# Gate ranks in one chunk, decays by bias on ScalarE, one AND for the causal mask, and a reordered start

## The reference

```python
h = rmsnorm(x_lat, norm1_g[i]) * (1.0 + sc1) + sh1          # sc1, sh1: from silu(c) @ ada_w
log_gate = log_sigmoid((lr @ gate_w[d] + gate_b[d])) / GLA_TAU   # lr: 16 columns of h @ w_in per direction
# linear attention, chunks of 64 tokens, forward and backward, 4 heads
b = cumsum(g)                                   # within the chunk
qe, ke, kd = q * exp(b), k * exp(-b), k * exp(b_last - b)
att = where(mask, qe @ ke.T, 0);  o = att @ v + qe @ S
S = exp(b_last) * S + kd.T @ v
# latent attention, 8 heads: softmax(q @ k.T) @ v; then pooling, three gated branches, w_out
# PEER: for each token and each of 8 heads the top 16 of 16384 experts
out = sum_j softmax(top)_j * gelu(x . u[eid_j]) * v[eid_j]
```

## Time and profile before

| what | value |
|---|---|
| median of 3 runs | 3509.55 us (3503.07 to 3510.31) |
| profiled execution, its own time | 3512.18 us |
| span of the profiled execution | 3510.2 us |
| PE, PE weight load | 2868.5 us, 1793.2 us busy |
| VectorE, ScalarE, GpSimd | 1751.3 us, 1083.8 us, 862.1 us busy |
| HBM read | 1067.80 MB |

### The profile page before, as it was taken

The page is one execution under the profiler, slowest core; times in us unless marked ns, Lnnn a source line. Parts: engine busy times, 40 slices in busy tenths (PEclk is TensorE's granted clock), DMA queues, the critical chain, the costliest instruction groups (busy, mean ns, idle before and its releaser), DMA issues.

```text
span 3510.2 us, 42731 instructions
## 1 busy us (share of the span) xinstructions
PE 2868.5 (82%) x16338; PEld 1793.2 (51%) x16338; DVE 1751.3 (50%) x4345; ACT 1083.8 (31%) x3065; POOL 862.1 (25%) x772
## 2 busy tenths in 40 slices
PE   7999998988898999988776555699999985566555
PEld 5787887654555666664332111278888741111111
DVE  1323013557676555556676766423300256667664
ACT  1222102243555444323433323222310123222232
POOL 0000000323233333323334444200000034444442
PEclk9999999999999999999877867799999987767776
DMA  8654441988898999989989999732144199999996
GB/s 324 273 204 157 156 152 61 379 345 337 347 373 325 420 416 421 384 338 365 386 327 410 415 410 414 300 120 87 70 155 147 72 376 415 411 411 410 410 412 278
DMA packets 151107, 1071.64 MB, mean 305 GB/s; under 512 B 16564, under 2 KB 18228, under 8 KB 22520
## 3 DMA queue, kind: packets, MB, share of 16 engines
q0 software_dynamic: 110592, 805.36, 57.0%
q1 hardware_dynamic: 40312, 263.56, 19.6%
HBM read 1067.80 MB, written 1.05 MB: 304 GB/s over the span
## 4 chain that ended last, share of the span: by engine, by line
PE 53%; DMA 26%; DVE 10%; ACT 6%; issue 3%; POOL 2%; DVEq 0%; ACTq 0%; SPq 0%; POOLq 0%
PE bank L388 39%; DMA ring<-in_experts,eid 25%; PE bank L402 11%; DVE ring L1357 5%; POOL ring L1782 2%; ACT topk_work L909 1%; PE bank L484 1%; ACT topk_work L902 1%; ACT topk_work L899 1%; PE bank L415 1%; DVE state L1547 1%; ACT L899 1%; ACT h_even L967 0%; DVE topk_work L1327 0%; PE bank L608 0%
## 5 line engine op out<-in xcount | busy, mean ns | idle before, releaser
L1782 POOL DMA_INDIRECT ring<-in_experts,eid x768 | 861.9, 1122 | 2611.1 <-PE bank L402 1317.2
L402 PE MATMUL bank<-ring,topk_work 64*64 64x512 f32 x6144 | 992.8, 775 | 542.9 <-ACT topk_work L909 539.1
L1357 DVE CUSTOM_DVE_ANT_0 ring<-ring,h2tok 128x1024 f32<-128x1024 f32 x768 | 936.6, 1224 | 591.7 <-DMA ring<-in_experts,eid 583.4
L402 PEld LDWEIGHTS bank<-ring,topk_work 64*64 64x64 f32 x6144 | 237.3, 160 | 1189.7 <-ACT topk_work L909 888.3
L899 ACT ACTIVATE topk_work<-topk_work 128x2 f32<-128x2 f32 x384 | 77.9, 203 | 1153.1 <-DVE topk_work L1357 1152.5
L388 PE MATMUL bank<-h_even,weights 128*128 128x256 f32 (+1 forms) x1360 | 313.8, 390 | 11.7 <-ACT h_even L967 11.7
L388 PEld LDWEIGHTS bank<-h_even,weights 128*128 128x128 f32 (+1 forms) x1360 | 252.0, 187 | 79.1 <-issue 26.4
L388 PE MATMUL bank<-h_odd,weights 128*128 128x256 f32 (+1 forms) x1056 | 241.5, 385 | 0.8 <-DVE h_even L1566 0.8
L909 ACT ACTIVATE topk_work<-const,topk_work 128x64 f32<-128x64 f32 x768 | 226.0, 341 | 0.4 <-ACT topk_work L902 0.4
L388 PEld LDWEIGHTS bank<-h_odd,weights 128*128 128x128 f32 (+1 forms) x1056 | 196.2, 189 | 57.1 <-issue 26.9
L902 ACT ACTIVATE topk_work<-topk_work 128x1 f32<-128x1 f32 x768 | 184.6, 287 | 12.6
(11 more groups left out here) (230 smaller groups left out, 3096.3 us busy)
## 6 DMA issues: line engine op xcount, KB each, us to landing
weights<-in_quads SPq DMA_DIRECT2D x150, 1024.0 KB, 7.6
ring<-in_quads SPq DMA_DIRECT2D x85, 1024.0 KB, 4.8
ring<-in_experts,eid POOLq DMA_INDIRECT x768, 8.7
ring<-in_quads SPq DMA_DIRECT2D x6, 768.0 KB, 4.2
weights<-in_quads SPq DMA_DIRECT2D x6, 768.0 KB, 6.1
...
```

The source lines that it names most:

```text
L402: x = nc.tensor.matmul(acc[g][out, :], diag[mine, J % 4, :], ring[mine, J % RING, D + h * 512:D + (h + 1) * 512], start=first, stop=J % TI ...
L1357: v.tensor_tensor_reduce(row, row, h2tok[:, u // UNITS % 2, :], 1.0, 0.0, ALU.mult, ALU.add, dots[:, u % 2, j:j + 1]).then_inc(S["dot_done ...
L1782: pool.indirect_dma_start(ring[:, J % RING, :], None, d["experts"], bass.IndirectOffsetOnAxis(eid[:, u % 2, j:j + 1], 0)).then_inc(gathere ...
```

## The change

The two gate-rank projections become one of 32 columns, and one block of ranks with a row of ones feeds both directions; the gate weights get zero rows. PE waits for h chunk by chunk, at the ranks and at the transposes before PEER. The input is loaded in two halves, the second behind the first eight quads; the first four modulation vectors come in the order scale, scale, shift, shift; ScalarE waits for the shift vectors only before it adds them. The decay exp(b_last - b) is taken on ScalarE alone, by eight exponentials of 64 columns with b_last as bias. The mask is one AND with a table `keep` (128 KB, loaded once). ScalarE evicts the outputs of units 0 and 1. Latent passes skip the second state increment of units 2 and 3, which nobody reads. Latent attention goes head by head, and the matmuls with the values take both query blocks at once. The planner adds 0.1 for each job in pass 1. Line numbers shift by some 11 to 33.

```diff
-PACE = 1.0
+BESIDE, PACE = 0.1, 1.0
...
-MOD_FIRST = [(0, q) for q in range(4)]
+MOD_FIRST = [(0, q) for q in (2, 3, 0, 1)]
...
-    quads_of = logs["quads"]
+    quads_of, rows_at = logs["quads"], logs["rows"]
...
+        keep = sb("keep", [P, 2, P], U32)
...
+        ends = sb("ends", [P, 3, GLA_H, 2])
...
-        lr17 = E[0:RANK + 1, 2560:3072].rearrange("p (d t) -> p d t", d=2)
+        ranks = E[0:2 * RANK + 1, 2560:2816]
...
-        probT = (E[:, 1024:1536].rearrange("p (k t) -> p k t", k=4), E[:, 1536:2048].rearrange("p (k t) -> p k t", k=4))
+        probT = [E[:, m:m + 1024].rearrange("p (k t) -> p k t", k=4) for m in (1024, 2048)]
+        rstd1 = E[:, 1024:1280]
...
-            return [(t, h) for t in range(2) for h in range(MLA_H)]
+            return [(t, h) for h in range(MLA_H) for t in range(2)]
+
+        def increments(s, u):
+
+            return 1 if s and u >= 2 else 2
...
-            sp.dma_start(XT[:], d["xT"].rearrange("(c p) t -> p c t", p=P)).then_inc(x_landed, 16)
+            sp.dma_start(keep[:], d["keep"]).then_inc(const_landed, 16)
+            xT = d["xT"].rearrange("(c p) t -> p c t", p=P)
+            sp.dma_start(XT[:, :, span(0)], xT[:, :, span(0)]).then_inc(x_landed, 16)
             last, loads = {}, {}
-            for key, n, slot, done in quads_of:
+            for order, (key, n, slot, done) in enumerate(quads_of):
+                if order == 2 * len(MOD_FIRST):
+                    sp.dma_start(XT[:, :, span(1)], xT[:, :, span(1)]).then_inc(x_landed, 16)
...
+                rows_now[key] = cur["next"]
...
+                        if ready:
+                            pe.wait_ge(*at("h", ready, n, k))
...
-                    for m in range(2):
+                    for m in range(increments(p.s, u)):
...
-                def weigh(m):
-                    t, h = au[m]
-                    pe.wait_ge(*at("evicted", "pt", n, m))
-                    b = job("ao", n, m)
+                def weigh(h):
+                    for t in range(2):
+                        pe.wait_ge(*at("evicted", "pt", n, 2 * h + t))
+                    b = job("ao", n, h)
                     for k in range(nk):
                         v = (VVctok if k < 2 else VVltok)[:, k % 2, h * MV:h * MV + MV]
-                        x = mm(b[:, 0:P], v, probT[m % 2][:, k, :], k == 0, k == nk - 1)
-                    full(x, "ao", n, m)
+                        x = mm(b[:, 0:TS], v, probT[h % 2][:, k, :], k == 0, k == nk - 1)
+                    full(x, "ao", n, h)
 
                 pe.wait_ge(*at("evicted", "krd", n))
                 for q in range(4):
...
-                    if m >= 1:
-                        weigh(m - 1)
+                    if m and m % 2 == 0:
+                        weigh(m // 2 - 1)
...
+                pe.wait_ge(*at("evicted", "lr", n, 0))
                 for dd in range(2):
-                    pe.wait_ge(*at("evicted", "lr", n, dd))
                     for t in range(2):
                         b = job("z", n, dd, t)
-                        x = mm(b[:, :], lr17[:, dd, tokl(t)], w[:, dd, :], True, True)
...
-                for k in range(DC):
-                    pe.wait_ge(*at("h", "norm1", n, k))
                 w = quad(i, "lr", k=DC)
-                project(n, "lr", w, [(0, 0, RANK), (1, RANK, RANK)], h_of(n), DC)
+                project(n, "lr", w, [(0, 0, 2 * RANK)], h_of(n), DC, ready="norm1")
...
+                        if t == 0:
+                            pe.wait_ge(*at("h", "norm2", GROUP_PASS[g], m * 4 + c))
...
-                            cur["pace"] = PACE if g == 1 else 0.0
+                            cur["pace"] = (0.0, PACE, 0.0)[g]
...
+                if n == 1:
+                    cur["pace"] = BESIDE
...
+                rows_until(rows_at.get(key, 0))
...
+                    if p.n == 0 and name == "norm1" and c % 4 == 0:
+                        act.wait_ge(*at("evicted", "mod", 0, 2 * SH1 + c // 4))
...
-                    x = nc.scalar.activation(decay[:, u % 3, :, :].rearrange("p h c -> p (h c)"), last_of(b, u), ACT.Exp,
-                                             scale=1.0 / TAU)
-                    x.then_inc(*mark("act_step", ("enb", n, u)))
-                    act.wait_ge(*at("bdiff", n, u))
-                    nc.scalar.activation(gla_buf(u, GD), gla_buf(u, GD), ACT.Exp, scale=1.0 / TAU).then_inc(
-                        *mark("act_step", ("ekd", n, u)))
+                    nc.scalar.activation(decay[:, u % 3, :, :].rearrange("p h c -> p (h c)"), last_of(b, u), ACT.Exp,
+                                         scale=1.0 / TAU).then_inc(*mark("act_step", ("enb", n, u)))
+                    nc.scalar.activation(ends[:, u % 3, :, :].rearrange("p h c -> p (h c)"), last_of(b, u), ACT.Copy,
+                                         scale=1.0 / TAU).then_inc(*mark("act_step", ("ends", n, u)))
+                    act.wait_ge(*at("ends", n, u))
+                    for h in range(GLA_H):
+                        for c in range(2):
+                            mine = slice(c * CHUNK, (c + 1) * CHUNK)
+                            x = nc.scalar.activation(gla_buf(u, GD)[:, h, mine], bv[:, h, mine], ACT.Exp, scale=-1.0 / TAU,
+                                                     bias=ends[:, u % 3, h, c:c + 1])
+                    x.then_inc(*mark(ACT_EV, ("evicted", "b", n, u), ("ekd", n, u)))
...
+                def first_out(u):
+
+                    dd, t = units[u]
+                    for g in range(2):
+                        b = bank_of("o", n, u, g)
+                        x = nc.scalar.activation(tokens_of(gla_of(n))[:, t, g * 512:g * 512 + 512], b[:, :], ACT.Copy)
+                        x.then_inc(*mark(ACT_EV, ("evicted", "o", n, u, g), *([("o_first", n, t)] if g else [])))
 
...
+                    if p.full and u in (1, 2):
+                        first_out(u - 1)
...
-                def scale_keys_first(u):
-                    dd, t = units[u]
-                    b = bank_of("b", n, u)
-
-                    dve.wait_ge(*at("enb", n, u))
-                    blocks = b[:, :].rearrange("p (n t) -> p n t", t=CHUNK)
-                    last = CHUNK - 1 if dd == 0 else 0
-                    flatd = gla_buf(u, GD).rearrange("p h t -> p (h t)").rearrange("p (n t) -> p n t", t=CHUNK)
-                    v.tensor_copy(flatd[:, :, 0:CHUNK], blocks[:, :, last:last + 1].to_broadcast([P, 8, CHUNK])).then_inc(
-                        *mark("dve_step", ("blast", n, u)))
-                    dve.wait_ge(*at("blast", n, u))
-                    v.tensor_tensor(flatd, flatd, blocks, ALU.subtract).then_inc(
-                        *mark(DVE_EV, ("evicted", "b", n, u), ("bdiff", n, u)))
-
                 def scale_keys(u):
                     dd, t = units[u]
+                    rows_before("b", n, u)
+
+                    dve.wait_ge(*at("enb", n, u))
                     if p.full:
...
-                    v.tensor_scalar(ga, b[:, :].rearrange("p (h t) -> p h t", h=GLA_H), HUGE, -HUGE, ALU.min,
-                                    ALU.max).then_inc(*mark(DVE_EV, ("evicted", "att", n, u)))
-                    dve.wait_ge(*at("evicted", "att", n, u))
-                    v.tensor_tensor(ga, ga, tri[:, dd, :].unsqueeze(1).to_broadcast([P, GLA_H, P]), ALU.mult).then_inc(
-                        *mark("dve_step", ("gla_att", n, u)))
-
-                seen = set()
+                    v.tensor_tensor(ga.bitcast(U32), b[:, :].rearrange("p (h t) -> p h t", h=GLA_H).bitcast(U32),
+                                    keep[:, dd, :].unsqueeze(1).to_broadcast([P, GLA_H, P]), ALU.bitwise_and).then_inc(
...
-                    if not p.full:
+                    if not p.full or u < 2:
...
                         o = tokens_of(gla_of(n))[:, t, g * 512:g * 512 + 512]
-                        keys = [("evicted", "o", n, u, g)]
-                        if t in seen:
-                            if g:
-                                keys.append(("o_sum", n, t))
-                            else:
-                                dve.wait_ge(*at("o_first", n, t))
-                            v.tensor_tensor(o, o, b[:, :], ALU.add).then_inc(*mark(DVE_EV, *keys))
-                        else:
-                            if g:
-                                keys.append(("o_first", n, t))
-                            v.tensor_copy(o, b[:, :]).then_inc(*mark(DVE_EV, *keys))
-                    seen.add(t)
-
-                scale_keys_first(1)
+                        keys = [("evicted", "o", n, u, g)] + ([("o_sum", n, t)] if g else [])
+                        v.tensor_tensor(o, o, b[:, :], ALU.add).then_inc(*mark(DVE_EV, *keys))
+
                 scale_keys(1)
...
-                        carry(u - 1, 1)
+                        if increments(s, u - 1) == 2:
+                            carry(u - 1, 1)
...
-                    for i, q in MOD_FIRST:
+                    for i, q in MOD_FIRST[:2]:
```

(5 more changed lines are left out.)

77 lines of the change are left out of this document (41 added, 36 removed).

## The result

The changed kernel took **3477.32 us** (median of 6 runs, 3461.49 to 3485.52) where the kernel before took 3506.53 (median of 6, 3503.07 to 3510.31): ratio 0.9902, 95% interval 0.9879 to 0.9926. Its profiled run took 3464.96 us (span 3462.9, mean clock 0.904).

What follows compares the result with a forecast made beforehand. PE was taken to pace passes 0 and 3, DMA the tail and end of pass 2, with a mixed part between. Savings of 23.2 us outside it plus 11 inside, 34 off 3512.2, gave a 3476 median; 8-in-10 range 3453 to 3495.

Steps and rivals of the forecast that it cites:

- The start: Up to the next modulation vector: earlier weights, earlier scale and shifts, and 16 fewer rank instructions save 9 us.
- My bound from the slow row: Input load at the start: at 258 GB/s both halves cost 4.1 us instead of 2.5, taking back 3.2.
- Pass 3: Pass 3: 6.5 us saved at its start, 1.5 in the queries, 1.5 in linear attention.
- Queries of pass 0: Transposes before the queries of pass 0: seven of eight fit in the wait for the last chunk, saving 1.5 us.
- Clock: Lower clock behind the gate logits, 96 to 100 us: the dip may go (about 3.4 us) or stay; 1.7 taken.
- Latent attention of pass 0: Exponentials in pass 0: half of VectorE's copies go, at most 0.19 us for each of 16 units; 2 us taken.
- Decays: Linear attention: eight exponentials of 64 columns at 0.29 us each hold ScalarE 2.4 us.
- The first group: Mixed part up to the second group: 7.7 us of PE work removed, waits perhaps 2 less; 8 us gained.
- the moving is worth nothing by itself: First group: 18 us of matmuls moved behind pairs by the planner's 0.1 return later, gaining nothing unless waits shrink.
- Rival C: Mixed part: denser pairs reach PE ahead of their diagonals, 0.4 us more wait a pair, 3527 us; chance 0.04.
- The second group: Rows up to 2258 us: PE's 3.4 us is hidden behind waits for rows; lighter VectorE may give 3 us.
- signs of being wrong: Second group's first row moving by less than 13 us, diagonal waits beyond 75 us, or half inputs landing no sooner.

Runs made afterwards that it cites:

- Experiment 5: Changed kernel with the old start (modulation order 0 to 3, whole input ahead of all weights, no early scale or shift): 3485.75 us, ratio 0.9941.
- experiment 4: Changed kernel with latent passes computing the second state increment of units 2 and 3 again: 3480.99 us, ratio 0.9928.
- experiment 3: Changed kernel with the decays on two engines again (VectorE copy and difference, one ScalarE exponential): 3481.04 us, ratio 0.9939.
- experiment 6: Kernel before with only the changed decays, eight biased exponentials on ScalarE and no VectorE operation: 3508.47 us, ratio 0.9996.
- experiment 11: Changed kernel with latent attention unit by unit as before, value matmuls and evictions too: 3472.06 us, ratio 0.9917.
- experiment 7: Kernel before with only the planner's change in pass 1, 0.2 for each job where it added 0.1: 3523.62 us, ratio 1.0043.
- experiment 12: Changed kernel with the planner's 0.1 in pass 1 only up to latent attention, 0 from the pooling on: 3476.01 us, ratio 0.9924.
- experiment 9: Changed kernel with the gate ranks in two chunks of 16 columns again, gate weights without zero rows: 3497.51 us, ratio 0.9968.

## Why the total was right and two terms were not

**The start** (forecast 9, bounds 6 and 10): measured 11.5 at the next vector in the first profile, and 10.4 at the first k projection in the means of all profiles (41.5, before 51.9). Experiment 5 gives 3.7 of that to the order and the halves. The steps held: ranks at 33.27 forecast as 33.3. It went beyond the bound because the clock came up during the 16 ranks, which took 4.7 us and not 6.8, and because the half inputs cost nothing visible (3.8 us sooner). The Trainium skill (DMA: Bandwidth & Descriptors, the table at its head), by which 1 KB pieces lose nothing, fits that: 322 GB/s from 4 to 8 us with them, 258 with 2 KB. My bound from the slow row did not show itself. The clock part is chance: the first 15 rank instructions took 5.07 us in this profile, 3.42 in the second and 6.32 in that of experiment 4.

**Pass 3** (9.5): 11.8. Its start gave 3.0 by the waits and 3.9 by the count of ranks (23.19 us for the first rank and k instructions, now 19.31), 6.9 against 6.5. In linear attention, forecast 1.5, PE's wait for the second unit's keys fell from 2.51 to 1.12 us: 1.4, forecast 1.3. What the decays give in the whole pass is not settled: 2.8 by experiment 3, 5.5 to 10 by experiment 6, where one program differs by 6.6. That PE would still gain nothing from the skipped increments held.

**Queries of pass 0** (1.5): from 6.40 + 1.94 to 3.50 + 3.18, 1.7. **Clock** (1.7): no dip behind the gate logits in this profile, one of some 4 us at 0.57 in the second: between the two cases, as taken.

**Latent attention of pass 0** (2 gained): wrong in sign. The forecast step "half of the copies go ... at most 0.19 each" overlooked that one copy of 256 columns stands in the turn of two where a copy of 128 stood: two turns take 3.99 us, before 3.82. That is 1.4 us lost in 16 units; undoing it (experiment 11) gives 1.2 back, from 29.0 to 27.8.

**Decays**: 1.75 us for eight exponentials, forecast 2.4, so 0.22 us each and not 0.29. The 0.29 was mis-sized: it is half of a pair of diagonals that takes 0.59 us together, each 0.347 long, so that only one start in two is hidden. The exponentials take 0.327 each and start 0.20 apart. The estimate from the Trainium skill (ScalarE: Activation LUTs) of 2.0 was nearer. The 0.7 beside it, for the one operation of 512 columns, took the price with a pointer, which that operation does not have; the rows have 0.60 and 0.63.

**The first group** (8 gained, bounds -6 and 18): 5.3 lost, from few profiles; what is clear is that the 8 did not come. The waits, which were to shrink, grew by 11.5 us from row 0 to row 256. The removed work is not the step that failed: undone one by one, ranks and increments cost 4.2 and 4.6 us, booked at 3.4 and 3.0, though neither is clear of the scatter. What failed is two terms put at nothing. One is "the moving is worth nothing by itself": the 0.1 alone costs 18.7 us in the kernel before (experiment 7), and without it from the pooling on the changed kernel is 7.0 faster here (experiment 12). The other is latent attention by head, "nothing in passes 1 and 3": undoing it gives 7.7 us here (experiment 11). What stays open is how they combine. Taking the whole 0.1 out of the changed kernel gains nothing (911.4 with it, 915.7 without), and no single part undone brings the 18.7 us back; that the parts place the pairs together differently is a guess.

Rival C's mechanism is real in the kernel before, where 12.1 of the 18.7 us are waits for diagonals, but it was priced too high: 18.7 us is 0.15 us a pair, and C needed 0.27 to decide and named 0.4. That experiment 7's 3523.62 is near C's 3527 is chance, since C's figure was for the whole change.

**The second group** (3 gained, bounds -4 and 6): 13.8. The failed step is "PE's 3.4 us is hidden". It is hidden as work, but it moves the planner's clock, and that moves pairs in the linear attention of pass 2. Rows 320 to 336 alone take 12.2 us less (54.9 to 42.7, means), nearly the whole gain, and with the old places 9 of them are lost (experiment 9). The lighter chain of decays is worth 3 us in these 16 rows with the old places and 6.5 with the new; over the whole group it gave nothing by itself (experiment 6).

**The signs named.** First row 12.7 us sooner (forecast 13), ranks at 33.27: both came. The ranks of pass 3 begin 0.65 us behind the first shift, not "some 3 us", which disagreed with the sum's own 2274.1. The exponentials at 0.22 us missed 0.25 to 0.3. Of the signs of being wrong, the first profile stays just clear (row 256 13.4 us sooner, waits 74.1 against a limit of 75), and the second shows two: row 256 only 8.2 us sooner, and waits of 76.5. They point where the forecast failed, in the first group.

So that the sum came out is luck: the second group's gain, which nobody planned, paid for the first group's loss. With the parts undone one by one, what carries the result is the ranks in one chunk, by the whole time (3497.51), and the start and the waits by chunk, by the marks. Decays, increments, latent attention and the planner's 0.1 each change the whole time by less than can be told.
